# Two 1024x3072 modulation products of two vectors: narrow TensorE products replaced by VectorE row sums

## The reference, cut to what matters

```
sc, scc = silu(c), silu(c_ctx)                       # two vectors of 1024
for i in range(2):
    sh,  scl,  gt  = split(sc  @ mod_w[i] + mod_b[i], 3)     # mod_w[i]: 1024 x 3072
    shc, sclc, gtc = split(scc @ mod_w[i] + mod_b[i], 3)
    in_lat = rmsnorm(h_lat, norm_w[i]) * (1 + scl) + sh
    ...
```

## Time and profile before

| what | value |
|---|---|
| times of three runs | 2450.77, 2455.66, 2455.25 us |
| median of the three | 2455.25 us |
| span of the profiled execution | 2450.6 us |
| lowest run above that span | 0.17 us |
| VectorE busy / ScalarE busy / GpSimd busy | 57% / 31% / 58% of the span |

### The profile page before, as it was taken

One profiled execution on the slowest core, in us unless ns is written; L12 is line 12 of the kernel. 1 busy time (PEld: TensorE's weight loads), 2 busy tenths in 40 slices (PEclk: granted clock), 3 DMA queues, 4 the chain that ended last, 5 costly groups with the idle time before them and its releaser, 6 DMA issues.

```text
span 2450.6 us, 33199 instructions
## 1 busy us (share of the span) xinstructions
PE 2360.5 (96%) x12198; PEld 1929.6 (79%) x12198; DVE 1390.7 (57%) x1675; ACT 760.1 (31%) x1616; POOL 1409.9 (58%) x1248
## 2 busy tenths in 40 slices
PE   8989999999999999999998899999999998999998
PEld 6868877888777687788877898998998997776446
DVE  7855211234675641111357797797797798608654
ACT  3452110102332520110236434334334334533451
POOL 8726666677777276666774443443443442265785
PEclk9989999999999999999999999999999999999999
DMA  4311444323224034432233011011011012021111
GB/s 164 118 62 69 140 170 155 112 86 112 86 71 144 18 120 166 166 116 103 86 114 118 35 52 51 34 51 51 34 51 51 34 52 92 24 103 56 42 36 69
DMA packets 37998, 209.27 MB, mean 85 GB/s; under 512 B 5136, under 2 KB 9232, under 8 KB 15120
## 3 DMA queue, kind: packets, MB, share of 16 engines
q1 hardware_dynamic: 27600, 164.85, 19.2%
q10 hardware_dynamic: 10304, 43.07, 5.0%
HBM read 195.58 MB, written 7.34 MB: 83 GB/s over the span
## 4 chain that ended last, share of the span: by engine, by line
PE 76%; DVE 15%; issue 4%; ACT 3%; DMA 1%; POOL 1%; ACTq 0%; DVEq 0%; SPq 0%; POOLq 0%
PE ps L507 38%; PE ps L824 13%; PE ps L1070 5%; DVE convd L2374 3%; PE ps L1187 2%; PE ps L921 1%; PE ps L1169 1%; PE ps L943 1%; DVE convd L2388 1%; PE ps L534 1%; PE ps L715 1%; PE ps L960 1%; PE ps L930 1%; PE ps L1174 1%; PE ps L932 1%
## 5 line engine op out<-in xcount | busy, mean ns | idle before, releaser
L406 POOL TENSOR_SCALAR whi<-wraw 128x512 fp32r<-128x512 f32 x564 | 374.8, 692 | 968.9 <-PE ps L824 438.3
L410 POOL TENSOR_TENSOR wlo<-wraw,whi 128x512 fp32r<-128x512 f32 x568 | 861.4, 1547 | 1.0 <-ACT whi L1432 1.0
L507 PE MATMUL ps<-uhi,whi 128*128 128x512 f32 x896 | 354.9, 396 | 16.0 <-POOL wlo L392 11.6
L507 PE MATMUL ps<-uhi,wlo 128*128 128x512 f32 x896 | 349.9, 390 | 0.0
L507 PE MATMUL ps<-ulo,whi 128*128 128x512 f32 x896 | 349.6, 390 | 0.0
L824 PE MATMUL ps<-inhi,whi 128*128 128x384 f32 (+1 forms) x784 | 243.5, 345 | 5.6 <-DVE inlo L2318 4.3
L824 PE MATMUL ps<-inhi,wlo 128*128 128x384 f32 (+1 forms) x784 | 236.2, 336 | 0.0
L824 PE MATMUL ps<-inlo,whi 128*128 128x384 f32 (+1 forms) x784 | 236.2, 336 | 0.0
L2207 DVE TENSOR_TENSOR h<-h,ps 128x1024 f32<-128x1024 f32 x40 | 48.8, 1221 | 306.8 <-PE ps L507 306.8
L507 PEld LDWEIGHTS ps<-uhi,whi 128*128 128x128 f32 x896 | 168.7, 188 | 59.1 <-POOL wlo L392 11.6
L507 PE MATMUL ps<-hidhi,whi 128*128 128x512 f32 x512 | 201.0, 393 | 0.0
(11 more groups left out here) (453 smaller groups left out, 4621.6 us busy)
## 6 DMA issues: line engine op xcount, KB each, us to landing
wraw<-in_wstream SPq DMA_DIRECT2D x150, 1024.0 KB, 4.8
modraw<-in_modw ACTq DMA_DIRECT2D x24, 1024.0 KB, 4.8
hspill<-hres ACTq DMA_DIRECT2D x1, 3072.0 KB, 10.9
hback<-hspill ACTq DMA_DIRECT2D x1, 3072.0 KB, 10.2
Q<-qrow SPq DMA_DIRECT2D x24, 128.0 KB, 2.3
h<-in_x ACTq DMA_DIRECT2D x2, 1024.0 KB, 5.2
QL<-qrest SPq DMA_DIRECT2D x14, 128.0 KB, 2.3
gw<-in_gates ACTq DMA_DIRECT2D x2, 512.0 KB, 3.5
```

The source lines that it names most:

```text
L406: pool.tensor_scalar(whi[:, s, c], wraw[:, s, c], 1.0, 0.0, ALU.mult, ALU.add).then_inc(wraw_read, 1)
L410: ins = pool.tensor_tensor(wlo[:, s, c], wraw[:, s, c], whi[:, s, c].bitcast(F32), ALU.subtract)
L507: mm = pe.matmul(ps[:, 2 * bank + m, :], a[:, w, c:c + P], b[:, kb, :], start=(n == 0 and i == 0), stop=(n == KB - 1 and i == 2))
```

## The change

The weights are laid out anew, with outputs on partitions: one block is 128 outputs x 1024 inputs (512 KB), 24 blocks per layer (`MODS` = 24), and `modraw` becomes two slots of that size, each with its own semaphore. TensorE does nothing for the modulation any more. Both vectors are broadcast to all partitions (`crow`, 128x2048), ScalarE takes their tanh at n = 1, and VectorE writes silu (times two) into PSUM banks 4 to 7 at n = 2. Then, for n = 4 to 27, VectorE does block m = n - 4: two `tensor_tensor_reduce` passes, one per vector, each multiplying the block with a row of PSUM, halving, and adding up along the row into one column of `modsb`. This happens once in each layer, the silu too.

```diff
-MODW = 2 * P
-MODS = 3 * D // MODW
+MODS = 3 * D // P
...
-    modraw = at("modraw", 184, [P, KB, MODW])
+    modraw = at("modraw", 184, [P, 2, D])
+    crow = at("crow", 144, [P, 2 * D])
+    ctanh = at("ctanh", 152, [P, 2 * D])
+    modprod = [at(f"modprod{i}", 160 + 4 * i, [P, D]) for i in range(2)]
```

On TensorE `mod_block`, `mod_turn` and `modulation` are gone, with their calls after each MLP tile:

```diff
-                    modulation(8 * c + j)
...
-                    modulation(8 * c + 4 + j)
```

On ScalarE:

```diff
             def mod_fetch(m):
-                act.dma_start(modraw[:, :, :], io["modw"][l * MODS + m]).then_inc(L["mod_dma"], 16)
+                act.dma_start(modraw[:, m % 2, :], io["modw"][l * MODS + m]).then_inc(L[f"mod_dma{m % 2}"], 16)
             def modulation(n):
                 m = n - MOD_AT
-                if 1 <= m <= MODS:
-                    act.wait_ge(L["mod_T"], l * PER["mod_T"] + m)
-                    A(modsb[:, 2 * (l * MODS + m - 1):2 * (l * MODS + m), :].rearrange("p a b -> p (a b)"), ps[:, 4, 0:4], ACT.Copy).then_inc(L["mod_ev"], 1)
-                if 0 <= m < MODS:
-                    act.wait_ge(L["mod_ps"], l * PER["mod_ps"] + m + 1)
-                    A(modrow[:, :], ps[:, 5, 0:MODW], ACT.Copy).then_inc(L["mod_row"], 1)
-                    if m + 1 < MODS:
-                        mod_fetch(m + 1)
+                if n == 1:
+                    act.wait_ge(lw[1], l * 32 + 32)
+                    A(ctanh[:, :], crow[:, :], ACT.Tanh, scale=0.5).then_inc(L["mod_row"], 1)
+                if 1 <= m < MODS - 1:
+                    act.wait_ge(L["mod_ev"], l * PER["mod_ev"] + m)
+                    mod_fetch(m + 1)
...
-            act.wait_ge(lw[1], l * 16 + 16)
+            act.wait_ge(lw[1], l * 32 + 16)
+            act.dma_start(crow[:, :], io["crow"].partition_broadcast(P)).then_inc(lw[1], 16)
             A(phi[:, :, :], pT[:, :, :], ACT.Copy).then_inc(L["phi_r"], 1)
...
             mod_fetch(0)
+            mod_fetch(1)
...
-                    fetch_gates(l + 1)
                     lru_rates(l + 1)
+            act.wait_ge(L["mod_ev"], l * PER["mod_ev"] + MODS)
             if l < DEPTH - 1:
+                fetch_gates(l + 1)
                 fetch_p(l + 1)
```

On VectorE:

```diff
-            if l == 0:
-                silu_c()
+            def modulation(n):
+                m = n - MOD_AT
+                if n == 2:
+                    dve.wait_ge(L["mod_row"], l * PER["mod_row"] + 1)
+                    V.scalar_tensor_tensor(out=ps[:, 4:8, :].rearrange("p a n -> p (a n)"), in0=ctanh[:, :], scalar=1.0,
+                                           in1=crow[:, :], op0=ALU.add, op1=ALU.mult).then_inc(L["mod_row"], 1)
+                if 0 <= m < MODS:
+                    w = modraw[:, m % 2, :]
+                    dve.wait_ge(L[f"mod_dma{m % 2}"], l * PER["mod_dma0"] + 16 * (m // 2 + 1))
+                    dve.wait_ge(L["mod_row"], l * PER["mod_row"] + 2)
+                    for v, out in enumerate((modprod[m % 2][:, :], w)):
+                        ins = V.tensor_tensor_reduce(out, w, ps[:, 4 + 2 * v:6 + 2 * v, :].rearrange("p a n -> p (a n)"), 0.5, 0.0,
+                                                     ALU.mult, ALU.add, modsb[:, l * MODS + m, v:v + 1])
+                    ins.then_inc(L["mod_ev"], 1)
...
-            V.memset(ps[:, 5, 0:MODW], 0.0).then_inc(L["p_r"], 1)
...
                                            op0=ALU.max, op1=ALU.mult).then_inc(L["m_r"], 1)
+                    modulation(8 * c + j)
                     dve.wait_ge(L["sqh_r"], l * PER["sqh_r"] + 2 * n + 2)
...
                     add_to_h(j, j % 2, T_MLP + 8 * c + 4 + j, 4 + 4 * c + j + 1)
+                    modulation(8 * c + 4 + j)
```

More of the change, by code:

```diff
@@ L135, in build @@
     modsb = at("modsb", 205, [P, 48, 2])
-    cvec = at("cvec", 205.375, [P, KB, 2])
     misc = at("misc", 206.75, [P, 16])
-    modrow = at("modrow", 206.8125, [P, MODW])
     xc = at("xc", 136, [P, 4, S])
@@ L347, in _ @@
             sp.dma_start(dst[:, :], io["consts"][:, a:b]).then_inc(cst2, 16)
-        sp.dma_start(cvec[:, :, :], io["cvec"]).then_inc(cst2, 16)
         with sp.Fori(1, (T_ATT + 13) // 2) as i:
@@ L522, in norm_sum @@
             mm.then_inc(L["ssq_r"], 1)
[L524 to L551, removed]
-            if 1 <= m <= MODS:
-                mod_turn(m - 1)
-            if 0 <= m < MODS:
-                mod_block(m)
         for l in range(DEPTH):
@@ L593, in rate_columns @@
                 pe.wait_ge(L["gate_t"], l * PER["gate_t"] + 8)
-                pe.wait_ge(cst2, 16 * 4)
+                pe.wait_ge(cst2, 16 * 3)
                 for t in range(4):
@@ L1386, in _ @@
             A(gt[:, :, :], gt[:, :, :], ACT.Tanh).then_inc(L["lru_a"], 1)
-            if l == 0:
-                act.wait_ge(cst2, 16 * 4)
-                A(csil[:, :], cvec[:, :, :].rearrange("p a b -> p (a b)"), ACT.Tanh, scale=0.5).then_inc(init_a, 1)
             act.wait_ge(L["lru_d"], l * PER["lru_d"] + 2)
@@ L1939, in angles @@
         def angles():
-            dve.wait_ge(cst2, 16 * 4)
+            dve.wait_ge(cst2, 16 * 3)
             init(V.tensor_copy(angt[0][:, :], posi[:, :]))
@@ L1952, in angles @@
             init(V.tensor_copy(maskb[:, :], maskf[:, :]))
-        def silu_c():
-            dve.wait_ge(init_a, 1)
-            cv = cvec[:, :, :].rearrange("p a b -> p (a b)")
-            init(V.scalar_tensor_tensor(out=cv, in0=csil[:, :], scalar=1.0, in1=cv, op0=ALU.add, op1=ALU.mult))
-            init(V.tensor_scalar(cv, cv, 0.5, None, ALU.mult))
         def norm_gain(i):
@@ L1968, in second_params @@
             dve.wait_ge(ld2, 7 * 16)
+            dve.wait_ge(L["mod_ev"], DEPTH * PER["mod_ev"])
             gf = p2[:, C2_GF:C2_GF + KB]
@@ L2147, in _ @@
             if l == 0:
-                dve.wait_ge(init_a, 4)
+                dve.wait_ge(init_a, 3)
                 init(V.tensor_scalar(ropeS[:, :], ropeS[:, :], misc[:, 3:4], None, ALU.mult))
@@ L3061, in host_arrays @@
         "positions": i["positions"].reshape(S),
-        "cvec": np.ascontiguousarray(np.stack([columns(i["c_2"][0]), columns(i["c_ctx_2"])], 2)),
+        "crow": np.concatenate([i["c_2"][0], i["c_ctx_2"]]),
         "lparams": np.ascontiguousarray(np.stack([layer_params(i, l) for l in range(DEPTH)], 1)),
```

21 lines of the change are left out of this document (8 added, 13 removed).

## The result

| kernel | median us | runs us | span of its profiled execution |
|---|---|---|---|
| before | 2455.45 | 2450.77 to 2457.42 (4) | 2450.6 |
| after | 2416.55 | 2415.92 to 2421.1 (4) | 2414.5 |

The ratio is 0.9849 with a 95% interval of 0.9837 to 0.9861: 38.9 us less by the medians. The forecast was 2417.8 us, in a range of 2411 to 2428.

What follows compares the result with a forecast made beforehand. TensorE alone was taken to bound the first part's MLP. Removing its small matmuls gives -37.65 us, silu's delay of GpSimd +0.2, passes nothing: 2455.25 - 37.45 = 2417.8 us, range 2411 to 2428 us.

Steps and rivals of the forecast that it cites:

- What bounds the MLP, and what goes: First part's MLP, both layers: TensorE alone bounds it; removing blocks, turns and slower tiles behind them gives back 37.65 us.
- A pass: VectorE: 1.22 us per pass plus 0.17 us for writing the sum, 2.8 us per slot, 134 us in all, hidden.
- the scan: Far bound for a pass's speed on VectorE: 2.39 us for 1024 elements at best, 4.40 us by its median.
- The 2.6 us at which I let stalls start: Slow row sum rival on VectorE: stalls start at 2.6 us a pass; with some stall 2425 to 2459 us, chance 0.06.
- The deadline: First down tile of a chunk: TensorE reads the last hidlo blocks at 8.17 us; hidlo ends at 5.8, 2.4 to spare.
- GpSimd: GpSimd's splits beside the passes: passes cost nothing, splits stay 5.03 us in down tiles and 6.0 in up tiles.
- the split with `gm` inside: GpSimd split at 621.93 us: 5.05 us with a 1.23 us PSUM-and-SBUF instruction inside, 5.03 undisturbed, so passes cost nothing.
- The rival with 8.4 us: Passes hold GpSimd off, making it the bound in up slots: 8.4 us more, 2426.2 us, chance 0.07.
- Silu: Silu instruction at n = 2, two SBUF operands, 2.29 us: delays GpSimd's split, 0.1 us per layer, bounds 0 to 0.6.
- The small run of instructions at the border of chunks 2 and 3: VectorE, layer 0, next layer's small instructions: the 2.8 us of passes make hm about 1.5 us late, at no cost.
- ScalarE and the transfers: Tanh of 1.92 us, 1.28 us table loads and half-size weight transfers stay hidden; uncovered, the root's load costs 1.28 us.
- The base: Whole kernel: the gain is subtracted from the median of 2455.25 us, 4.65 us above the profiled execution.

Runs made afterwards that it cites:

- no_turns: Kernel before without the 24 turns (pairs of 2-column matmuls), modsb filled from a constant, modulation left out: 2445.29 us, ratio 0.9959 to before.
- no_blocks: Kernel before without the 24 blocks (eight narrow matmuls each over modraw), modulation left out: 2427.99 us, ratio 0.9891 to before.
- passes_x3: Changed kernel with every pass made three times, each extra one waited for, same result: 2428.41 us.
- passes_x3_but_last: Changed kernel with every pass made three times, except once only in the last up tile of each chunk: 2415.11 us.
- no_passes: Changed kernel without its 96 row sums, a two-element memset in place of each pair: 2415.84 us, ratio 0.9843 to before.
- sbuf: Changed kernel with silu written to SBUF instead of PSUM, so passes read two SBUF operands: 2419.87 us, ratio 0.9861 to before.

## Why the prediction was right

**What bounds the MLP, and what goes.** Right. 37.65 us were read off the chain; the MLPs gave 38.02. The 0.37 are 1% of the term; measured slots of 10.88 us instead of the 10.887 of the earlier trace rows make up less than half of it, and the rest isn't traced. no_turns and no_blocks confirm the parts: each piece's length, and a slower tile behind it. That the whole kernel came within 1.3 us of the forecast is in part luck, as its runs scatter over 5 us; the MLPs are the test.

**A pass.** 1.22 us, the price of the add to `h` and 1.17 by the reduction's rate; measured 1.216 and 1.215. The nearest rows were the right ones and the scan was not. (The 2.6 us at which I let stalls start include the writing of the sum; a pass alone could take 2.4, the scan's best, and no more.) Writing out the sum takes 0.08 us, half of what I took. Four instructions with their overlaps make 2.28 us, not 2.8, so `hidlo` ended 5.0 us behind the tile's end where I had 5.8. VectorE's busy time rose by 1498.1 - 1390.7 = 107.4 us where I had 134.

**The deadline.** The 8.17 us, read from the code and the tile's length alone, is confirmed by passes_x3 to 0.1 us (369.69 by it, 369.62 by the rhythm of the matmuls), and passes_x3_but_last shows that of the slots with passes it's the only kind with a deadline that six passes break.

**GpSimd.** Nothing from the passes: right, and the row that carried it, the split with `gm` inside, was enough. The rival with 8.4 us falls with no_passes and passes_x3. By the rule of the Trainium skill that I had set beside it ("SBUF — State Buffer", Who interferes with whom) this was to come out so, and sbuf shows its other side: with two SBUF operands the same instruction takes 1.97 us per pair from GpSimd.

**Silu.** I took 0.1 us per layer out of 0 to 0.6. The instruction and the `hidlo` behind it took 3.0 us from the split, and the split ended just in time, with the weight load 0.17 us late and the matmul on its beat. My working put the whole 2.3 us on top of the usual up slot and came out 0.2 over; 5.38 + 5.03 against the usual 2.38 + 6.02 is 2.0 more, and those 0.3 us decide. So it costs nothing that shows, but by a margin that I couldn't have foretold; its price is read from this one slot, and no run leaves it out.

**The small run of instructions at the border of chunks 2 and 3.** Wrong, without effect. I said that 2.8 us of passes in front would make `hm` 1.5 us late. The run's end and `hm` in the changed kernel:

```profile
502.35 0.17 DVE L1969 TENSOR_SCALAR small<-lpall 128x8 f32<-128x8 f32 x1
503.46 1.23 DVE L2195 SCALAR_TENSOR_TENSOR hm<-ps,rstd 128x1024 f32<-128x1024 f32 x1 [0.94 <-PE ps L505]
```

VectorE still waited 0.94 us for TensorE there, against 1.33 before. The run had started 2.3 us later in its slot and caught up 1.8; how is told in the last section.

**ScalarE and the transfers.** Hidden, as said; VectorE never waits for `modraw`, and the 512 KB land in 3.3 us. The table load for the third norm's root comes earlier than the root. One wait I had not named: behind the fetches ScalarE does the small rates of the next layer, and now stands there for 33.41 us until a pair of passes is done. The trace has nobody who waits for it.

**The base.** I set the gain on the median and called the 4.65 us between it and the profiled run noise. That was right, and where much of it comes from can be seen now (last section).

## What to carry to other kernels

If the chain of waits shows small TensorE pieces between long tiles, their cost is their length in the chain and what they slow the tile behind them (here 0.26 us on 1.31, a fifth more), and it comes back whole when the work moves to an engine with room. Room isn't idle share: add up where the moved work stands in its slot, up to the one consumer with a deadline (here `hidlo` at a chunk's border), and put it elsewhere in that one slot if it doesn't fit. Where VectorE runs beside a GpSimd without much slack, keep one operand of VectorE's long instructions in PSUM: the same work cost nothing so, and made the kernel slower than before with both operands in SBUF once there were four passes to a slot.
